# Mixture-of-experts products: from three split fp32r matmuls a tile to plain float32 matmuls on four column tiles of 32, straight on the landed weight panels

## What is computed

```python
def moe_swiglu(h, w_router, w_gate, w_up, w_down):
    t = h.reshape(-1, dm)                                  # 256 tokens x 1024
    logits = t @ w_router                                  # 256 x 8
    top_v, top_i = lax.top_k(logits, 2)
    gates = jax.nn.softmax(top_v, axis=-1)
    comb = jnp.sum(jax.nn.one_hot(top_i, 8) * gates[..., None], axis=1)
    for e in range(8):
        out = out + comb[:, e:e+1] * ((silu(t @ w_gate[e]) * (t @ w_up[e])) @ w_down[e])
```

## Time and profile before

| | us |
|---|---|
| median of 3 runs (1707.25 to 1708.89) | 1707.36 |
| span of the profiled execution | 1705.2 |
| PE busy in it | 1625.6 (95%) |
| DVE busy | 1271.7 (75%) |
| ACT busy | 1041.4 (61%) |
| mixture of experts, from its first product (719.5) to its last (1691.3) | 971.8 |

### The profile page before, as it was taken

How to read it: one execution, slowest core, us unless ns; L and a number is a source line. 1 busy time by engine, 2 the same in 40 slices (tenths; PEclk the granted TensorE clock), 3 DMA queues, 4 the chain that set the end, 5 groups by cost and what they waited for, 6 DMA issues and landing times.

```text
span 1705.2 us, 23552 instructions
## 1 busy us (share of the span) xinstructions
PE 1625.6 (95%) x9115; PEld 1364.1 (80%) x9115; DVE 1271.7 (75%) x1142; ACT 1041.4 (61%) x1034; POOL 194.8 (11%) x152
## 2 busy tenths in 40 slices
PE   8799999998999988989999999999999999999996
PEld 7679999877878767778888888888888888888884
DVE  5644444485847564678888888888888888888886
ACT  5453443554546453367777777777777777777773
POOL 0100000124423333010101001001001001010100
PEclk9799999999999999999999999999999999999999
DMA  9146555542222100589999999999999999999992
GB/s 349 58 141 210 176 191 177 173 138 91 69 100 75 50 1 2 221 292 405 373 373 378 381 383 375 376 379 371 378 378 374 367 388 369 378 375 379 378 404 103
DMA packets 158991, 450.97 MB, mean 264 GB/s; under 512 B 9648, under 2 KB 40784, under 8 KB 158928
## 3 DMA queue, kind: packets, MB, share of 16 engines
q1 hardware_dynamic: 155392, 436.96, 69.5%
q0 software_dynamic: 3536, 13.11, 2.0%
HBM read 441.66 MB, written 8.39 MB: 264 GB/s over the span
## 4 chain that ended last, share of the span: by engine, by line
PE 86%; DVE 7%; ACT 3%; issue 1%; SPq 1%; POOL 1%; DMA 1%; DVEq 0%; POOLq 0%; ACTq 0%
PE bank L1433 26%; PE bank L1435 25%; PE bank L1434 25%; PE bank L1824 1%; PE bank L1935 1%; PE bank L1834 1%; ACT whi L584 1%; DVE wlo L927 1%; DMA par<-in_attn_sinks_dram 1%; DVE wlo L1240 1%; DVE TT L1198 1%; DVE cvall L1107 1%; PE bank L1816 1%; PE bank L1862 0%; PE bank L1841 0%
## 5 line engine op out<-in xcount | busy, mean ns | idle before, releaser
L1240 DVE TENSOR_TENSOR wlo<-raw,whi 128x2048 fp32r<-128x2048 f32 x336 | 766.9, 2290 | 110.1 <-ACT whi L815 107.5
L815 ACT CAST whi<-raw 128x2048 fp32r<-128x2048 f32 x336 | 643.4, 1915 | 250.8 <-PE bank L1435 247.7
L1433 PE MATMUL bank<-whi,xhi 128*128 128x512 f32 (+1 forms) x1584 | 575.9, 364 | 11.4 <-DVE wlo L1240 2.9
L1435 PE MATMUL bank<-whi,xlo 128*128 128x512 f32 (+1 forms) x1584 | 567.8, 358 | 0.0
L1434 PE MATMUL bank<-wlo,xhi 128*128 128x512 f32 (+1 forms) x1584 | 567.1, 358 | 0.0
L1433 PEld LDWEIGHTS bank<-whi,xhi 128*128 128x128 f32 x1584 | 300.0, 189 | 59.8 <-issue 4.8
L1435 PEld LDWEIGHTS bank<-whi,xlo 128*128 128x128 f32 x1584 | 300.1, 189 | 44.2
L1434 PEld LDWEIGHTS bank<-wlo,xhi 128*128 128x128 f32 x1584 | 300.3, 190 | 41.3
L927 DVE TENSOR_TENSOR wlo<-raw,whi 128x2048 fp32r<-128x2048 f32 x74 | 178.5, 2415 | 80.3 <-ACT whi L584 80.0
L1433 PE MATMUL bank<-whi,ehhi 128*128 128x512 f32 x448 | 178.9, 399 | 5.4 <-DVE wlo L1240 3.9
L1435 PE MATMUL bank<-whi,ehlo 128*128 128x512 f32 x448 | 177.4, 396 | 0.0
(11 more groups left out here) (304 smaller groups left out, 1546.3 us busy)
## 6 DMA issues: line engine op xcount, KB each, us to landing
raw<-in_moe_w_gate_dram SPq DMA_DIRECT2D x112, 1024.0 KB, 6.8
raw<-in_moe_w_up_dram SPq DMA_DIRECT2D x112, 1024.0 KB, 6.6
raw<-in_moe_w_down_dram SPq DMA_DIRECT2D x112, 1024.0 KB, 7.2
raw<-in_dn_w_in_dram SPq DMA_DIRECT2D x24, 1024.0 KB, 5.2
raw<-in_ffn_w_gate_dram SPq DMA_DIRECT2D x11, 1024.0 KB, 5.5
raw<-in_ffn_w_up_dram SPq DMA_DIRECT2D x11, 1024.0 KB, 6.1
raw<-in_ffn_w_down_dram SPq DMA_DIRECT2D x11, 1024.0 KB, 5.0
raw<-in_dn_w_o_dram SPq DMA_DIRECT2D x8, 1024.0 KB, 5.1
```

The source lines that it names most:

```text
L815: act.copy(slot(whi, n, SPLIT), slot(raw, n, RAW)).then_inc(hi_ready, 1)
L1240: dve.tensor_tensor(slot(wlo, n, SPLIT), slot(raw, n, RAW), slot(whi, n, SPLIT).bitcast(F32), ALU.subtract).then_inc(lo_ready, 1)
L1433: pe.matmul(ps, lhs_hi, wh, start=start, stop=False)
L1435: return pe.matmul(ps, lhs_lo, wh, start=False, stop=stop)
```

## The change

Only the mixture of experts is changed. Its panels are no longer split: PE takes them as plain float32 moving operands from where they landed. The stationary operand is 128 x 32 (one tile of 32 tokens), the output goes to 32 partitions, and four matmuls on the four column tiles take four different quarters of the panel's columns. 3 token tiles x 32 = 96 tokens are handled in a pass (`npass` goes up to 3). The space of the split buffers becomes a ring of 14 panels, freed by `panel_used`. Transposed hidden values are 6 (3) instead of 8 (4). Expert rows lie in quarters over partitions, so one indirect DMA becomes three; the last rows come to their tokens by 24 float32 matmuls of 32 rows. DVE's list for the row numbers grows (`over1`, `over2`, `pos32`, `dest`, `tilerow`).

```diff
-RAW, SPLIT = 6, 3
+TILE, TILES = 32, 3
+SLOTS = TILE * TILES
+PASSES = -(-SEQ // SLOTS)
+RING = 14
+    ring = [at(f"ring{n}", PANEL, kb) for n, kb in enumerate((96, 104, 24, 32, 40, 0, 8, 16, 48, 72, 56, 80, 64, 88))]
 # SP
             def head():
-                for i in range(HEAD):
+                for i in range(RING):
+                    if i < 2:
+                        sp.wait_ge(panel_used, PROJ[GROUPS - 1, 5] + 1)
+                    elif i < 8:
+                        sp.wait_ge(lo_ready, P_MOE - 6 + i - 2 + 1)
+                    else:
+                        sp.wait_ge(panel_used, P_MOE - 3 + (i - 8) // 2 + 1)
             def body(e, it, following):
                 def panel_of(i, src):
-                    expert_panel(B_MOE + i, it * EP + (B_MOE + i - RAW + 1), src)
+                    sp.wait_ge(panel_used, it * EP + (B_MOE + i - RING + 1))
+                    expert_panel(B_MOE + i, src)
 # POOL
-                pool.indirect_dma_start(y_rows, ... yrow[:, :], None)
+                for t in range(TILES):
+                    pool.indirect_dma_start(y_rows.rearrange("r (q c) -> (r q) c", q=4), ... yrow[:, t * 256:(t + 1) * 256], None)
 # ACT: ehi, hidden_hi, gathered_hi gone; instead
+            def hidden_sb(u, wide_):
+                act.wait_ge(sem("ehT_psum"), u + 1)
+                    act.copy(ehT[:, 0:512], bank[6])
+                    i = act.copy(ehT[:, 512:768], bank[7][:, 0:256])
 # DVE: elo, hidden_lo, gathered_lo gone
             def body(it, last):
-                lo_upto(0, 3)
-                hidden_lo(it * ECH, True)
...
-                hidden(it * ECH + 1, used(D0), True)
+                hidden(it * ECH + 1, used(U1 + 4), True)
...
-                hidden(it * ECH + 3, used(D2), False)
+                hidden(it * ECH + 3, used(U3 + 2), False)
                 if last:
                     add_chosen()
-                    lo_upto(31, D3_LAST + 2)
-                    hidden_lo(it * ECH + 3, False)
                     return
 # PE
+            def token_tile(first, t, q, width):
+                at_ = t * width
+                return bank[first + at_ // 512][TILE * q:TILE * (q + 1), at_ % 512:at_ % 512 + width]
             def gate_up(n0, done, first, end):
                 for j in range(first, end):
                     m, i = divmod(j, 4)
                     n = n0 + j
-                    pe.wait_ge(lo_ready, done * EP + (n + 1))
+                    pe.wait_ge(*expert_landed(n, done))
+                    w = expert_slot(n)
                     for k in range(2):
                         kt = 2 * i + k
-                        for h in range(2):
-                            at_ = k * 1024 + h * 512
-                            last = triple(bank[2 * m + h], *gxT(kt), n, slice(at_, at_ + 512), kt == 0, kt == KT - 1)
+                        for t in range(TILES):
+                            for q in range(4):
+                                at_ = k * 1024 + q * 256
+                                last = pe.matmul(token_tile(2 * m, t, q, 256), xg[:, kt, TILE * t:TILE * (t + 1)], w[:, at_:at_ + 256],
+                                                 start=kt == 0 and t % 2 == 0, stop=kt == KT - 1, skip_group_check=t % 2 == 1)
             def down(...):        # the same, with ehT[:, h_:h_ + TILE]; the half-width chunk takes 48 matmuls of 128 columns a panel
-                        for h in range(2):
-                            i = triple(bank[4 + h], ehhi[:, s_], ehlo[:, s_], n, ...)
+                        for t in range(TILES):
+                            for q in range(4):
+                                i = pe.matmul(token_tile(4, t, q, 256), ehT[:, h_:h_ + TILE], w[:, at_:at_ + 256], ...)
 # PE, behind the last turn
-            for h in range(2):
-                pe.wait_ge(sem("last_ylo_ready"), h + 1)
-                    pe.matmul(bank[LAST_BANKS[2 * h + b]], t_, yhi[:, s_], start=True, stop=False)
-                    pe.matmul(bank[LAST_BANKS[2 * h + b]], t_, ylo[:, s_], start=False, stop=True)
+            pe.wait_ge(sem("ylast_ready"), 1)
+            for b in range(TB):
+                for q in range(4):
+                    for t in range(TILES):
+                        i = pe.matmul(bank[LAST_BANKS[4 * b + q]][:, 0:256], selTr[p_, ...], ylast[p_, t * 256:(t + 1) * 256], ...)
```

More of the change, by code:

```diff
@@ L201, in trunk @@
     lg, top, oh1, oh2, tmp8 = (small(TB * NE) for _ in range(5))
-    pos, cmb = (small(TB * (TURNS + 1)).rearrange("p (b e) -> p b e", b=TB) for _ in range(2))
+    pos = small(TB * (TURNS + 1)).rearrange("p (b e) -> p b e", b=TB)
+    cmb = small(TB)
     topi = small(TB * NE)
@@ L227, in sem @@
             return sems[name]
-        landed = [sem(f"panel_landed{n}") for n in range(RAW)]
+        landed = [sem(f"landed{n}") for n in range(RING)]
+        LANDED_ONCE = (16, 16, 16, 16, 16, 48, 48, 32)
+        x_loaded, x_late, ident_loaded, first_half_landed, tab_loaded, bias_loaded, loads, phase_b_params = landed[RAW:]
         hi_ready, lo_ready, panel_used = sem("hi_ready"), sem("lo_ready"), sem("panel_used")
[L231 to L234, removed]
+        gain_loaded = sem("gain_loaded")
         panels = []
@@ L291, in trunk, with expert_slot, expert_landed @@
         EP = FFE // 256 * 3
-        assert EP % RAW == 0 and EP % SPLIT == 0
+        assert EP % RING == 0 and P_MOE % RAW == 3 and P_MOE % SPLIT == 0
         HEAD = 8
         B_MOE = P_MOE + HEAD
+        AHEAD_OF_LOOP = RING - HEAD
+        dense_landed = [16 * len(range(n, P_MOE, RAW)) for n in range(RAW)] + list(LANDED_ONCE)
+        def expert_slot(n):
+            return ring[(n - P_MOE) % RING]
+        def expert_landed(n, done):
+            r = n - P_MOE
+            return landed[r % RING], done * (16 * EP // RING) + (dense_landed[r % RING] + 16 * (r // RING + 1))
         G1, U1, D0, G2, U2, D1, G3, U3, D2, GN, UN, D3 = 0, 4, 8, 12, 16, 20, 24, 26, 28, 32, 36, 40
@@ L881, in body @@
                 silu(used(UN), True)
-                hi_upto(39, EP)
-            for i in range(2):
-                ehi(P_MOE + i, 0)
             act.wait_ge(sem("route_dve"), 1)
@@ L1928, in row_numbers @@
                 for b in range(TB):
-                    i = pe.matmul(bank[6][:, 0:TURNS + 1], sel[:, b, :].bitcast(F32), rowno[:, b, :], start=b == 0, stop=b == TB - 1)
+                    pe.matmul(bank[6][:, 0:NE], sel[:, b, :].bitcast(F32), rowno[:, b, :], start=b == 0, stop=b == TB - 1)
+                for b in range(TB):
+                    i = pe.matmul(bank[6][:, NE:NE + TURNS * TILES], sel32[:, b, :], tilerow[:, b, :, :].rearrange("p e t -> p (e t)"),
+                                  start=b == 0, stop=b == TB - 1)
                 i.then_inc(sem("numbers_psum"), 1)
```

364 lines of the change are left out of this document (171 added, 193 removed).

## The result

The change makes the kernel slower: 1740.3 us (median of 4 runs, 1736.2 to 1745.1) against 1708.1 for the kernel before (median of 4 runs, of which the table above has three), ratio 1.019 (95% interval 1.017 to 1.021). The profiled execution has a span of 1738.5 us, 33.3 above the one before.

The account below looks back on a forecast made before the run. PE was taken to bound the kernel. Turns -29.4, last expert -3.1, head -4.8 and tail -0.4 make -37.7; with +24 for loop edges, span 1705.2 becomes 1691.5, and with 2.2 for the median 1694 us, range 1664 to 1728.

Parts of the forecast that it names:

- A panel's price: Expert panel on PE: 48 passes on four column tiles at once, 12 pitches, 2.59 us against 2.72 before.
- the rival of two or three tiles: Expert panels on PE: only two or three column tiles run at once, about 2565 or 1980 us; chance 0.16.
- A turn: One turn of the expert loop without its edge: -4.2 us, to 115.5 us; seven turns -29.4.
- the six switches between column tiles and the whole array: PE, six times a turn: 0.29 us for each pair of switches, +1.7 us a turn.
- The loop's back edge: Refetch of PE's larger loop body at six taken edges: 2.5 us plus 1.5 of half clock, 4.0 each, +24 us.
- my two bounds: Transfers used to price the edge's fetch: a plain 64 KB one, 1.9 us, and the gather beside panel traffic, 10.1 us.
- the edges are dear: Rival at the loop's edges: over 5.7 us each, by a fetch in several steps; up to 1739 us; chance 0.14.
- The narrow chunk: Narrow chunk's panels on PE: 24 pitches of 0.109, 2.6 us each, with an instruction issued every 13.5 ns.
- a stall at places other than the edge: Sign in the profile after that would show the prediction wrong: PE stalling elsewhere than at the loop's edge; no size given.
- The head's waits for DVE: First expert: PE's wait of 1.79 us ahead of the fifth panel and 1.4 of half clock go; head -4.8 in all.
- The tail: Last turn and combining: waits gone -5.9, last expert's way to its tokens by float32 matmuls +5.5, together -0.4 us.
- Covered work: Hidden chain, three scatters, gather and panel DMA in the loop: hidden behind PE's panels, counted at nothing.

Follow-up runs that it names:

- e5: The change with PE's loop of seven turns written out and the narrow chunk's gate and up products done together by 256 columns; 1654.9 us, ratio 0.970.
- e1: The change with PE's loop of seven turns written out, so no branch on PE; 1691.4 us, ratio 0.992 to the kernel before.
- e3: The change with the narrow chunk's gate and up products together, 96 matmuls of 256 columns for 192 of 128; 1710.1 us, ratio 1.002 to the kernel before.
- e7: The change with each panel behind the first 14 loaded only in part, PE's work the same; 1681.4 us (one run).
- e8: The kernel before with each product of the experts' panels in two matmuls of 256 columns instead of one of 512; 1771.3 us, ratio 1.038.
- e10: The kernel before with only the wide gate and up products in two matmuls of 256 columns; 1745.6 us, ratio 1.022.
- e2: The change with PE's loop kept and its back edge hinted; 1703.9 us, ratio 0.999 to the kernel before.

## Why the prediction was wrong, point by point

I said 1694 us in 1664 to 1728, and faster with 0.69. It is 1740.3, slower, for which I gave 0.23.

**A panel's price: right.** 12 pitches of 0.216, 2.59 us, was predicted and measured. The records start in rounds of four, 6 to 7 ns apart, every 0.216 us (every 0.109 in the narrow chunk). Four tiles are four times as fast; the rival of two or three tiles, and with it the strict reading of the rule in the Trainium skill ("TensorE: Matmul & The Clock Gate", Part 3), that matmuls start and end in program order, is out. With two passes a matmul, each of the four tiles starts its first pass before the first tile's second.

**A turn: right, but for two terms that are not work.** I had 115.5 us without the edge. e5 has 114.9 with 0.3 of added transposes, so 114.6. The 0.9 us between are the six switches between column tiles and the whole array, which I had at 1.7: the products' stretches in a turn of e5 sum to 109.6 us where 42 x 2.59 is 108.9, so all the switches cost some 0.7.

**The loop's back edge: mechanism right, size half.** The step that failed is "among panel traffic I take 2.5, and with a half clock of 1.5 behind it, 4.0 an edge". It is 7.9 (e1 against the change, and e3 against e5: 122.8 - 114.9), of which 6.9 is the branch's own and 1.0 is lost in the chunks (e1, and the last section). My 2.5 was drawn from a transfer of 64 KB that took 1.9 us, and that one was the first of the program: DMA moved 55 GB/s on average in the first 3 us. e7 shows that 4.1 is right for an edge with a third of the traffic. Of my two bounds, 1.9 and 10.1 us, only the gather's 10.1 had moved beside the traffic in question, and I took a value close to the other one; the idle time alone is 5.1. It is 6 x 3.9 = 23 us of the miss, and the case stood among the rivals as "the edges are dear" (over 5.7, chance 0.14, up to 1739).

**The narrow chunk: a term that was missing.** "24 pitches of 0.109, the rate is shown to within a tenth" asked only whether PE can start an instruction every 13.5 ns. It can: the last turn shows 10.5 us. I never asked whether instructions come that fast. At 13.5 ns, 256 of them last 3.5 us, and in this stretch of the change packets come 4.3 to 5.1 us apart (they start at 944.2, 949.3, 953.8 and 958.1 us in the turn shown). In the last turn, where the panels have landed, they start 3.6 to 4.1 us apart and PE has no hole. The term is 4.6 us a turn (the change against e3, whose three added transposes are in it), 30 us of the median; it was in no rival, though "a stall at places other than the edge" stood among the signs of being wrong. With both sizes right, my own sum would read 1670 + 6 x 7.9 + 30 = 1747, where 1740 is measured; the cheaper tail (4 us, below) and switches (7 turns of 0.9 us) are of about that size.

**The ends.** The head's waits for DVE went as predicted, and from the first product to the loop's first row numbers the kernel is now 7.8 us faster (85.8 to 78.0 us by the two timelines). The tail was priced too high. From the last product to the end it was 13.9 us and is 15.4: +1.5, not +5.5. The combination, 48 passes,

```profile
1724.41 5.35 PE L2021 MATMUL bank<-ylast,selTr 32*128 32x256 f32 x48 [0.98 <-ACT ylast L875]
```

takes 5.35 us and not 8.7 to 10.4: matmuls of the next quarter's rows start beside those of this one, although they stand behind them in the program, so about two run at a time. The first quarter has six passes, and its last one, the first to count `last_comb_psum`, is the tenth record to start (1725.60 us).

**Covered work: right.** For PE no wait for a landing, for DVE or ACT is listed in the loop; the scatters, the gather and the hidden chain are hidden, in e5 even at 114.9 us a turn.

## What to carry to other kernels

Count instructions as a stream of their own, with two questions: does the loop's body stay on the engine, and how long do 256 instructions last where they are shortest? If a block lasts less than a fetch takes beside the traffic of that stretch, the engine starves though nothing else is late, and wider instructions for the same columns get it back. An idle stretch with releaser "issue" at a loop's head or in a run of short matmuls, together with instruction packets in every turn, is how it looks; price it by transfers that moved beside the same traffic, never by one that was alone.

## What the runs showed that I had not expected

- A fetch depends on the traffic that it stands beside: the stretch at the head is 5.1 us at 355 GB/s and 2.6 at 116, on average.
- A body of 1,720 instructions already comes anew in each turn, one of 1,140 doesn't. One and a half to two packets more than the body fills are fetched a turn (19 where some 4,500 instructions fill 17.6, 10 where 2,150 fill 8.4, 9 where 1,720 fill 6.7), as if it were read on beyond the branch.
- The same miss costs less idle time in e8 and e10 (2.8 and 1.0 us) than in the change (5.1), at about the same traffic (351 and 363 GB/s, 355). The instructions ahead of the branch last 0.06 us each in e8, 0.11 in e10 and 0.027 in the change, so work already issued may cover more of it. The packets fit: the one that ends the stretch starts 2.4 us after PE has stopped in the change, 0.2 after in e8 and 1.5 before in e10. No run takes it apart.
- In e1 and e2 the first chunk of the body takes 21.7 us where it takes 20.7 in e5, at a clock of 1.00; in every turn three rounds of four, 5 to 7 us into it, come 0.3 to 0.5 us apart instead of 0.216. They are there without any branch, so of the 7.9 us by which e3 is longer than e5 a turn, 1.0 is not the edge's. What they are stays open.
